# A hybrid decoder trunk on one core: a conv tap and a head scaling move from VectorE to ScalarE, and three issue points move

## The reference

```
x = x + 0.5 * ffn1(rmsnorm(x))                    # SwiGLU, hidden width 2816
u = rmsnorm(x);  [q k v g p c gates] = u @ W_in   # 13 blocks of 512 columns
y_ret  = (retention(q, k, v) * silu(g)) @ W_ret_out   # 4 heads, each head normalised by its rms
y_pool = block-diagonal map of causal means of p
a, b = split(c);  w = a * sigmoid(b)
y = causal depthwise conv of w, 31 taps, 512 channels, + bias
y_conv = silu(layernorm(y)) @ W_conv_out
x = x + (sig(g_ret)*y_ret + sig(g_pool)*y_pool + sig(g_conv)*y_conv) @ W_out
x = x + 0.5 * ffn2(rmsnorm(x))
```

## Time and profile before

| | |
|---|---|
| median of 3 runs | 1127.97 us |
| the profiled execution | 1128.66 us, its span 1126.9 us |
| TensorE busy | 1119.3 us, 99% of the span |
| TensorE's weight loads | 926.2 us, 82%, beside its matmuls |
| VectorE busy | 803.1 us, 71% |
| ScalarE busy | 649.7 us, 58% |
| GpSimd busy | 30.6 us, 3% |
| granted TensorE clock | 0.998 of full speed |
| DMA | 244.65 MB, 217 GB/s |

### The profile page before, as it was taken

The page is one execution under the profiler, slowest core; times in us unless marked ns, Lnnn a source line. Parts: engine busy times, 40 slices in busy tenths (PEclk is TensorE's granted clock), DMA queues, the critical chain, the costliest instruction groups (busy, mean ns, idle before and its releaser), DMA issues.

```text
span 1126.9 us, 13064 instructions
## 1 busy us (share of the span) xinstructions
PE 1119.3 (99%) x5006; PEld 926.2 (82%) x5006; DVE 803.1 (71%) x985; ACT 649.7 (58%) x744; POOL 30.6 (3%) x68
## 2 busy tenths in 40 slices
PE   9999999999999999999999999999999999999997
PEld 7888888888888878888888888888888888888886
DVE  6856565899998775655476655478999987665543
ACT  7755545763657675554475554376637476756442
POOL 0100000000100000000000000000001001000000
PEclk9999999999999999999999999999999999999999
DMA  9896666763756787656587656467637677867551
GB/s 357 311 271 209 215 241 192 248 206 118 258 215 192 210 286 208 222 187 224 159 279 261 216 192 229 176 213 251 199 122 266 238 193 224 269 220 224 159 187 38
DMA packets 130862, 244.65 MB, mean 217 GB/s; under 512 B 99040, under 2 KB 100448, under 8 KB 106224
## 3 DMA queue, kind: packets, MB, share of 16 engines
q1 hardware_dynamic: 128016, 236.61, 63.8%
q0 software_dynamic: 1648, 6.06, 1.5%
q10 hardware_dynamic: 1136, 1.15, 0.3%
HBM read 219.16 MB, written 1.05 MB: 195 GB/s over the span
## 4 chain that ended last, share of the span: by engine, by line
PE 97%; DMA 1%; DVE 1%; ACT 0%; SPq 0%; issue 0%; POOLq 0%; POOL 0%; DVEq 0%; ACTq 0%
PE acc L419 31%; PE acc L421 31%; PE acc L420 31%; DMA xT_planes<-x_planes 1%; PE acc L463 1%; PE acc L468 1%; PE acc L472 1%; PE ret L684 0%; PE tr L595 0%; PE tr L604 0%; DMA hT_planes<-h_planes 0%; PE tr L513 0%; DVE xT_lo L1302 0%; DVE hT_whole L1293 0%; DVE w_lo L1248 0%; ACT xT_hi L851 0%
## 5 line engine op out<-in xcount | busy, mean ns | idle before, releaser
L1248 DVE TENSOR_TENSOR w_lo<-raw,w_hi 128x2048 fp32r<-128x2048 f32 (+2 forms) x204 | 445.3, 2213 | 87.0 <-ACT w_hi L817 87.0
L817 ACT CAST w_hi<-raw 128x2048 fp32r<-128x2048 f32 (+2 forms) x204 | 375.1, 1849 | 212.2 <-PE acc L421 206.0
L419 PE MATMUL acc<-w_hi,xT_hi 128*128 128x512 f32 x1152 | 450.8, 391 | 0.6 <-DVE xT_lo L1302 0.6
L421 PE MATMUL acc<-w_hi,xT_lo 128*128 128x512 f32 x1152 | 448.5, 389 | 0.0
L420 PE MATMUL acc<-w_lo,xT_hi 128*128 128x512 f32 x1152 | 448.2, 389 | 0.0
L419 PEld LDWEIGHTS acc<-w_hi,xT_hi 128*128 128x128 f32 x1152 | 216.3, 188 | 45.7 <-DVE xT_lo L1302 1.0
L421 PEld LDWEIGHTS acc<-w_hi,xT_lo 128*128 128x128 f32 x1152 | 216.2, 188 | 45.3
L420 PEld LDWEIGHTS acc<-w_lo,xT_hi 128*128 128x128 f32 x1152 | 216.4, 188 | 44.0
L1331 DVE SCALAR_TENSOR_TENSOR h<-acc,rs,silu_gate 128x256 f32<-128x256 f32 x88 | 42.5, 483 | 148.1 <-ACT silu_gate L884 148.1
L419 PE MATMUL acc<-w_hi,hT_hi 128*128 128x512 f32 x348 | 135.4, 389 | 0.0
L420 PE MATMUL acc<-w_lo,hT_hi 128*128 128x512 f32 x348 | 135.4, 389 | 0.0
(11 more groups left out here) (144 smaller groups left out, 649.7 us busy)
## 6 DMA issues: line engine op xcount, KB each, us to landing
raw<-in_weights SPq DMA_DIRECT2D x192, 1024.0 KB, 5.1
raw<-in_weights SPq DMA_DIRECT2D x20, 256.0 KB, 5.7
raw<-in_weights SPq DMA_DIRECT2D x8, 512.0 KB, 3.4
bias<-in_gate_bias POOLq DMA_DIRECT2D x6, 512.0 KB, 5.5
x<-in_x SPq DMA_DIRECT2D x2, 512.0 KB, 10.7
scale_row<-in_pool_scale POOLq DMA_DIRECT2D x2, 512.0 KB, 5.9
hT_planes<-h_planes SPq DMA_TRANSPOSE x54, 3.1
band<-in_band POOLq DMA_DIRECT2D x1, 768.0 KB, 6.8
```

Of the source, the lines that this page charges most:

```text
L419: nc.tensor.matmul(o, a_hi, b_hi, start=first, stop=False)
L421: return nc.tensor.matmul(o, a_lo, b_hi, start=False, stop=last)
L817: nc.scalar.copy(w_hi[:, hf % HIGHS, 0:n], raw[:, hf % RAWS, 0:n]).then_inc(hi_split, 1)
L1248: nc.vector.tensor_tensor(w_lo[:, hf % RAWS, 0:n], raw[:, hf % RAWS, 0:n], w_hi[:, hf % HIGHS, 0:n].bitcast(F32), ALU.subtract).then_inc(l ...
```

## The change

It has four parts. (1) ScalarE makes the conv's first tap, bias included, as four ACTIVATE instructions of 128 x 256 behind `u_out`; VectorE begins with the second tap, and the numbers of taps at four places in its order change (8 to 10, 5 to 3, the last four to none). (2) ScalarE multiplies retention's heads by their factor (eight ACTIVATE of 128 x 128, PSUM to SBUF), and VectorE's eight instructions become two multiplications of 128 x 512. (3) The transposes of the conv's sums stand two product steps earlier in TensorE's order. (4) In SP's order the turn of (t = 1, c = 1) of each seam comes right behind that of (t = 1, c = 0), ahead of the load of half 4.

```diff
                 in_block(l, M_GATE_CONV, 0)
-                in_block(l, M_GATE_CONV, 1, mid={4: lambda: turn_y(l, 0), 5: lambda: turn_y(l, 1)})
+                in_block(l, M_GATE_CONV, 1, mid={2: lambda: turn_y(l, 0), 3: lambda: turn_y(l, 1)})
...
-                        for ahead, t, c in ((2, 0, 0), (2, 0, 1), (3, 1, 0), (4, 1, 1)):
+                        for ahead, t, c in ((2, 0, 0), (2, 0, 1), (3, 1, 0), (3, 1, 1)):
                             if hf % HALVES == 2 * at + ahead:
                                 turn_x(hf // HALVES, norm, t, c)
...
+            def first_tap(l):
+                act.wait_ge(u_whole, l * T + T)
+                act.wait_ge(pad_zero, l + 1)
+                for c in range(CH):
+                    w = PAR_CONV_W + c * TAPS
+                    nc.scalar.activation(y[:, c, :], uT[:, c, 0:S], ACT.Identity,
+                                         bias=par[:, l, PAR_CONV_B + c:PAR_CONV_B + c + 1],
+                                         scale=par[:, l, w:w + 1]).then_inc(conv_step, 1)
...
+            def scale_ret(l, t):
+                act.wait_ge(head_rs_ready, l + 1)
+                act.wait_ge(u_split, l * T + t + 1)
+                for hd in range(HEADS):
+                    s = slice(hd * P, (hd + 1) * P)
+                    a = nc.scalar.activation(ua[:, t, s], ret[:, t, s], ACT.Copy,
+                                             scale=head_rs[:, t, hd:hd + 1])
+                a.then_inc(ret_scaled, 1)
...
                 u_out(l, 0)
                 u_out(l, 1)
+                first_tap(l)
                 cast(ahead(M_Q) + 1)
...
                 gate_tanh(l, POOLED, 1, 0)
+                scale_ret(l, 0)
+                scale_ret(l, 1)
 
                 cast(ahead(M_POOL))
                 gate_tanh(l, POOLED, 1, 1)
...
-                    if i >= CH:
-                        dve.wait_ge(conv_step, l * (CH * TAPS) + i - CH + 1)
-                    else:
-                        dve.wait_ge(u_whole, l * T + T)
+                    dve.wait_ge(conv_step, l * (CH * TAPS) + max(CH, i - CH + 1))
...
-                dve.wait_ge(head_rs_ready, l + 1)
-                for hd in range(HEADS):
-                    s = slice(hd * P, (hd + 1) * P)
-                    a = nc.vector.scalar_tensor_tensor(ua[:, t, s], ret[:, t, s],
-                                                       head_rs[:, t, hd:hd + 1],
-                                                       g_silu[:, t, s], ALU.mult, ALU.mult)
-                a.then_inc(ret_ready, 1)
+                dve.wait_ge(ret_scaled, l * T + t + 1)
+                nc.vector.tensor_tensor(ua[:, t, :], ua[:, t, :], g_silu[:, t, :], ALU.mult
+                                        ).then_inc(ret_ready, 1)
...
-                taps_done[0] = 0
+                taps_done[0] = CH
...
                 gate_z(l, RET, 0, 0)
-                conv_taps(l, 8)
+                conv_taps(l, 10)
...
                 merge(l, RET, 0, 1, merged_ret)
-                conv_taps(l, 5)
+                conv_taps(l, 3)
```

More of the change, by code:

```diff
@@ L288, in trunk @@
         head_rs_ready = sem("head_rs_ready")
+        ret_scaled = sem("ret_scaled")
         ret_ready = sem("ret_ready")
@@ L1469, in conv_taps @@
                     k, c = divmod(i, CH)
-                    if i >= CH:
-                        dve.wait_ge(conv_step, l * (CH * TAPS) + i - CH + 1)
-                    else:
-                        dve.wait_ge(u_whole, l * T + T)
+                    dve.wait_ge(conv_step, l * (CH * TAPS) + max(CH, i - CH + 1))
                     w = PAR_CONV_W + c * TAPS + k
[L1475 to L1483, removed]
+                    nc.vector.scalar_tensor_tensor(y[:, c, :], uT[:, c, k:k + S], par[:, l, w:w + 1],
+                                                   y[:, c, :], ALU.mult, ALU.add
+                                                   ).then_inc(conv_step, 1)
                     taps_done[0] += 1
```

## The result

The changed kernel takes 1132.2 us (median of 15 runs, 1128.8 to 1136.0) against 1128.0 (1127.5 to 1129.9) for the kernel before: ratio 1.003, 95% interval 1.002 to 1.0039. I had said 1128.5, and a range up to 1130.2. It is slower, by more than the range allowed, and its times scatter over 7 us where those of before scatter over 2.4. The profiled execution took 1134.25, span 1132.4, so it is one of the long ones. Two runs of the kernel before that stand beside the experiments, of 1405.8 and 1641.3 us, were taken in a slow state and are left out.

What follows compares the result with a forecast made beforehand. TensorE, busy 1119.3 of 1126.9 us, was taken as the bound. Part 1's losses 0.97 and 0.49, less part 2's 0.10 and part 4's 0.81, gave +0.55 on the median 1127.97: 1128.5, range 1127.0 to 1130.2.

Steps and rivals of the forecast that it cites:

- Part 1, layer 0: VectorE's rotary step after ScalarE's first taps: 1.79 us late, costing TensorE 0.72 at the load of the decayed scores.
- the 0.11 of a late load: At TensorE's weight loads: each late load was taken to cost 0.11 us less than its lateness.
- the bank: Bank of the second pooled sums, freed for the scores: slack 0.33 us, 0.25 more lost in layer 0, 0.24 in layer 1.
- The four first taps: ScalarE's four first taps at the conv: 2.13 us in all, bounds 1.77 and 2.81.
- Part 1, layer 1: Same rotary step in layer 1: taps begin at 773.88, step 1.32 us late, 0.25 lost at the decayed scores.
- ScalarE itself has caught up by then, since it waits for TensorE before most casts: Casts behind ScalarE's first taps: ScalarE's own lateness was expected to be made up, with no loss counted.
- The sum without a lag: Whole kernel: 0.97 + 0.49 - 0.10 - 0.81 = +0.55 us, giving 1128.5.
- the rival that TensorE waits for VectorE that is over 4 us late: At the conv's last tap: TensorE waits, costing the lateness beyond 4 us in both layers; chance 0.03.
- Part 4: Seam (0, 3): second turn lands sooner, gain 0.81 us, bounds 0 and 0.91; passed load starts about 1.8 later.
- Nothing is expected of the other four seams: Seams other than (0, 3): no gain from part 4, since the profile rows show no second wait of this kind.
- Part 2: Heads on ScalarE: merge of the retention product 0.07 us sooner, gain 0.05 a layer, 0.10 in all.
- Part 3: Transposes of the conv's sums, at 334.92 rather than 336.28: no cost, 4.2 us in hand, and no gain.

Runs made afterwards that it cites:

- rotary first: Changed kernel with VectorE's first four taps moved from ahead of its second tile's rotary step to the last place, part 3 undone: 1128.1 us, ratio 0.9997 to kernel before.
- experiment 5: Part 4 at one seam, against the kernel before: part 1 with (0, 3) 1129.6 us, part 1 with (1, 1) 1130.0; rotary first with (0, 3) 1128.5.
- Rotary first with the earlier turn: Rotary first (parts 1, 2, 4) with the turn of u's first tile issued one weight load sooner: 1128.2 us, ratio 0.9997 to the kernel before.

## Why the prediction was wrong

- **Part 1, layer 0: right.** Late by 1.69 (1.79 said), of which 1.08 was absorbed (0.38, 0.58 and the 0.11 of a late load make 1.07). Loss 0.61 rather than 0.72, and 0.26 at the bank, as said. The four first taps took 2.08, not 2.13. By the Trainium skill, "ScalarE: Activation LUTs", section "What ACT_TABLE_LOAD costs", my estimate had been 2.06, and the trace agrees with it better than with my sum.
- **Part 1, layer 1: the step that failed.** "In layer 1, 557.80 later, it had waited 1.04 there, so the taps began at 773.88, and the same sum gives 1.32 late." The start was taken from one execution, in which u's turn landed in time, as if it were a property of the kernel. With such a landing the term is right: 1.21 to 1.36 late in three profiles, a stop of 0.12 to 0.27 and 0.22 to 0.28 at the bank. With a lag it is 2.9 to 4.7 in five profiles, a stop of 1.8 to 3.6, and behind the three longest of these stops 1.6 more for the clock. With VectorE's own taps the same lag costs far less, because VectorE has 1.04 in hand there and no 2.1 of ScalarE's taps behind the copy: the two such kernels with a lag of 3 lost 0.53 and 0.64 at `inner` and some 0.26 at the bank. ScalarE's own lateness I had at nothing too ("ScalarE itself has caught up by then, since it waits for TensorE before most casts"); by its casts it cost 0.37 in rotary first's profile.
- **The sum without a lag stands.** The nearest profile without one (parts 1, and 4 at seam (0, 3)) has 0.62, 0.23, -0.93, 0.27 and 0.28 at the five places, together +0.47, where my sum without part 2's -0.10 has +0.65. TensorE stood 0.55 more behind 920 us, which I hadn't in the sum, and so the change's best runs, 1128.8 to 1129.5, lie 0.3 to 1.0 above 1128.5. My range of 1127.0 to 1130.2 held five of the 15. Of the rival that TensorE waits for VectorE that is over 4 us late I wrote "Nothing in the rows makes it so late": that rested on the same single landing.
- **Part 4: right at its place, and optimistic in size.** -0.82 at seam (0, 3), as said; the load that is passed began 2.4 later, not 1.8. But the stop of 0.91 in the kernel before was a draw as well: with the old order it was 0.4 to 0.8 in four other traces, 0.66 on the mean of the five. Part 4 alone shows 0.5 in the median, within the noise. "Nothing is expected of the other four seams" holds, but its reason, that rows 2 show no second wait of this kind, was that of one trace (see the last point). Whether moving their loads makes lags more frequent stays open: with part 1, and part 4 at (1, 1), 19 of 35 runs were over 1131, without it 11 of 34, but in experiment 5, on one chip, it was 4 of 12 against 2 of 12. Why one DMA engine, if it is one, is behind in some executions and not in others is open too.
- **Part 2: right.** The scalings held nothing up; the merge gave back 0.11, as counted; with parts 2 and 4 the time is that of before. **Part 3: right**, no wait at the transposes.
- **Not foreseen:** 0.1 to 1.0 more than in the one trace of before at two places behind 920 us, in every other kernel's trace, rotary first included. One is the wait for a low part of weights at 926 us. The other is seam (1, 3), where the load waits 0.2 to 0.6 for the low part of x in 13 of the 17 traces, with either order of the turns, but not in that of before. What makes these waits is open.

No version beats the kernel before by more than the measurement tells. Rotary first with the earlier turn (1128.2) is merely steadier: none of its 11 runs was over 1128.5, of the kernel before beside it 9 of 25.

## What to carry to other kernels

Ahead of a step that must be punctual, don't put an operation that waits for a DMA, though in the profile at hand the DMA lands in time: take the wait's spread over runs, or over all transfers of that kind in the trace, as a term of the sum. An engine's idle time in front of a late input is an insurance, and moving the work that filled it to an engine behind the same input cancels it. And a change whose best runs match the forecast while its median doesn't may have a term that is drawn anew in each run.

## What the runs showed of the hardware

- Packets of a transposing DMA behind 1 MB loads on one queue can stay open for us and end together: 18 packets of 256 bytes of up to 3.6 us instead of 0.018, all ending within 0.04, 83 GB/s at a DMA share of 1.18. That they wait for the one DMA engine that is behind is my reading of the times. Such stays of 1.3 us and more are in every trace, 5 to 10 times, the kernel before's too (1.9 at 1034 us); at u's first turn in layer 1 they were there in 10 of the 17 traces, 1.6 to 3.6 long.
- TensorE's clock fell to its 1.2 GHz level behind stops of 2.10, 3.35 and 3.58 us, for 1.6 us of loss each time, and stayed at 2.4 behind stops of 1.47, 1.78 and 2.06. What decided between 2.06 and 2.10 is not shown.
